# New step orders for the engines in seven kinds of stages of a sixteen-stage transformer kernel on one core

## The chip, the cores and the metric

The kernel runs on one core of a Trainium2 chip. The metric is the device time of one execution in microseconds (us). Executions of this kernel agree closely, so two versions can be told apart from about 0.2% on.

## The reference

Two blocks of a language model in fp32 over 256 tokens of width 1024. The first block is four layers, each a SwiGLU feed-forward part, a mixer and a second SwiGLU part; the mixers are a gated delta rule (layers 1 and 4), stick-breaking attention and a sparse attention. The second block is twice a three-branch mixer and a squared-ReLU feed-forward part.

```
def rmsnorm(x, g): ...
def swiglu(h, w_gu, w_down):
    gate, up = jnp.split(h @ w_gu, 2, axis=-1)
    return (jax.nn.silu(gate) * up) @ w_down
...
def gated_deltanet(h, w_in, conv_w, a_log, dt_bias, norm_g, w_out):
    # causal depthwise conv and silu on q, k, v; q and k to unit length
    # chunk_gated_delta_rule: per chunk the inverse of a unit lower
    # triangular matrix, then products with q, k, v and the state
    ...
    return o.reshape(bsz, seq, GDN_DIM).astype(h.dtype) @ w_out
...
def mixer_sublayer(x, positions, w_in, ...):
    a, b, c = gla_branch(...), gmlp_branch(...), moba_branch(...)
    return (ga * a + gb * b + gc * c) @ w_out
```

Every stage is x + part(norm(x)). The output is x after the second block.

## The kernel before

The work is cut into sixteen stages: ffn1, gdn, ffn2, ffn1, sb, ffn2, ffn1, dsa, ffn2, ffn1, gdn, ffn2, mixer2, ff2, mixer2, ff2. Activations stay in SBUF all the time; the weights come from HBM piece by piece, up to 1 MB each, through the SP queue into a ring of five buffers (`RING`). Each fp32 weight piece is split in two: ScalarE writes its rounded high part `hi` (L638), VectorE writes the rest, `lo = raw - hi` (L656); for five pieces of each gdn stage and four of the dsa stage GpSimd does that subtraction (L676, `pool_split`). The activations are split likewise (`xh`, `xl`; L720 and L812). TensorE then makes three products for each block, hi by xh, lo by xh, hi by xl (L430, L431, L432 and, for column pieces, L503 to L505). The split of piece p + 3 stands at the first step of piece p. A split has to wait until its piece has landed, and hi(q) until TensorE has used piece q - 5.

The order on every engine is written out by hand in a script for each kind of stage: a string of names such as `W x1 W gate flip turn out norm next`. `run(script, lanes)` walks it and takes the next part of the generator with that name. On all engines `W` advances the weight pieces by one step; a split is issued at the `W` at which its piece is due:

```
def run(script, lanes):
    for step in script:
        if step in lanes:
            next(lanes[step])
```

No compiler reorders anything: the instructions of an engine execute in the order of its script, and each waits for semaphores of the data that it reads and of the buffer that it overwrites. A `W` that carries no split issues nothing on ScalarE, VectorE or GpSimd.

The steps that are spoken of below:

- ffn and ff2: `x1` and `next` transpose the activation (L541, L587) and split it; `gate` is silu on ScalarE (L1113) and a product on VectorE; `flip` (L993) and `turn` (L1017, L1028) take the hidden activation through DMAs issued by GpSimd (L1005, L1009); `out` adds the residual (L836), `norm` is L867 to L882.
- gdn: `E` is one step of the convolution, one VectorE product (L1604) and six taps (L1610), with two taps on ScalarE between (L1401). `inv` on GpSimd is the inversion by 31 pairs of row operations (L1797, L1800) between a VectorE transpose (L1719) and the VectorE steps L1724, L1726, L1728 (`inv` in `vector_gdn`). ScalarE copies that inverse into block form in sixteen operations (`MT`, L1401), and from there a chain of small products (L616) and VectorE steps (L1661) leads to the stage's output. `c0` to `c3` on GpSimd (L1782, L1784) clear and mask the four blocks of the chain. The first split on GpSimd waits for the last step of the convolution, `("conv", g, 22)`.

Of the kernel before, what the change touches and what calls it, by code (L numbers as in the profile page):

```python
# [1053 lines left out]
W W W W W W W next W W  # L1054
"""
FFN_ACT = """
x1 W W W W W W W gate W W W gate W W gate W turn turn W W gate W W W W turn W gate W W turn W W W gate W W W W gate
turn W W turn gate W W W W turn W gate W W W turn W gate W W W W turn gate W W W turn W W W W turn W W W W W W W W W W
W W W W next W W
"""  # L1060
FFN_DVE = """
x1 W W W W W gate W W flip W gate W W flip W W turn gate flip W W turn W gate W flip W W W turn W W gate flip W W W
turn W gate W flip W W W turn gate W flip W W turn W gate W flip turn W gate W W flip W W turn W gate W flip W W turn
gate W flip W W turn W W W W turn W W W out W W W W W W W W W W next out out W W W W
# [98 lines left out]


# [67 lines left out]


GDN_PE = """
x1 W W rbc rbc W W W W W gates W W W gates gates gates gates W W c0 W c2 nk nk nk c3 W nk c0 nk W W c1 c2 kT c1 c3 W W
W W W W W kT W W nq nq nq W nq W W nq W W qk qk rows W W rows rows rows qk W W c2 c0 c1 c0 c2 c0 c1 c0 c2 c1 a0 c3 c2
a0 c3 a0 c3 c1 a0 a1 a0 c3 a1 a1 qk a0 a0 a1 W a1 W W a1 a1 W W W W next W gates gates nk nq
"""
GDN_ACT = """
x1 W W W rbc rbc E E ba W W gates W W E gates W W gates W W E nk E W W nk W W nk gates gates gates E nk c0 c2 nk W  # L1240
W c0 c3 c2 c1 c3 c1 W W E kT E nq E W W nq E nq nq E W W W W nq W W E kT sv W W Z rows rows c2 c0 c3 c1 Z c2 c0
rows c1 rows gate W W c3 a0 a0 a0 W W a0 a0 a1 a1 a1 a0 a0 a1 a1 a1 a1 W W W W W W next W W W gates nk nq
"""
GDN_DVE = """
x1 clear rbc W W W E E gates W W gates E gates W W gates E W W gates gates W W E c2 c0 nk nk nk nk E c0 nk c3 W W
nk c2 c1 c3 c1 W W W W inv E E gates W W E W W nq nq nq E E W W nq E W W nq nq qk qk inv c1 c2 c0 qk c3 c0 c0 c2 c1
c0 c2 c1 a0 a0 c2 c3 a0 c3 c1 a0 a1 a0 a1 c3 a0 qk a1 a0 a1 a1 a1 a1 out W W W W W W W W W W W W out next W W out W
W W rbc
# [899 lines left out]
DSA_ACT = """
W W W x1 W p0 W normq W W W turn_q W normq normq p1 W normk turn_q W normk qi turn_q W normk normk W uq index_q
index_q index index index index index W index W index uv W turn_q uk normk turn_k W attention attention attention  # L2150
attention attention attention index W attention attention attention attention attention W W W attention index W W W
next W W W
"""
# [323 lines left out]


MIXER2_PE = """
W W x1 W x1 W W gla W W W W W W decays W W W W W W W decays decays W W W W W gla W decays decays W gla gmlp W gla gmlp  # L2480
gla W gmlp gla decays gla gla W gla decays W decays gla gla decays gla gla gmlp gla W gmlp gmlp gla W W gla W gmlp W W
W gmlp gmlp moba gla W moba W moba W gmlp W W moba W W W attention attention W W W attention attention W W W W W W W
attention W W attention W W W attention W W W W W W attention W W W W yT W W W W W W yT W W W W W W next next W
"""
MIXER2_ACT = """
W W decays x1 x1 W mu W W W W W W W mz W W W W gq W W W decays decays gk W decays decays W decays decays decays W W W
gla decays W gla gg gla W gla W gelu gla gla W gmlp W gla gla gmlp W W gla gla W oq gmlp W gla gmlp moba gla W gla W
gmlp gla gmlp W ok gmlp W gla W gla ov gmlp gla moba moba W W gmlp W W W moba gmlp W W sg attention W W W attention
attention W W W W attention sg W W W sg W attention W W W W W attention W W attention W W sg attention W W W norm sg W
W W W W yT W sg W W W yT W W W W norm next next W W W norm  # L2490
"""
MIXER2_DVE = """
clear x1 x1 W W W W W W W W lr angles W W decays W W angles W decays W W decays decays W decays W W gla W decays gla
gla decays W gv W gla W gla W gla gla decays decays gla W W W gla W gla W gla gmlp gla gla W gmlp gla gmlp gmlp W gmlp
gla gla W W gmlp W W gmlp gmlp gmlp moba W moba moba gla W W W W W W moba W gmlp attention W W y W W attention
attention W W attention W y attention W W W W y W W W W W attention W y W W W W attention W attention W W y W W W yT W
W y W yT W W W W W W norm out norm W next next out W W W norm
"""


# [683 lines left out]
```

## Time and profile before

| | us |
|---|---|
| median of three runs | 2890.73 (2890.49 to 2891.34) |
| span of the profiled execution | 2888.2 |
| PE busy | 2850.4 (99%) |
| DVE busy | 1794.7 (62%) |
| ACT busy | 1577.3 (55%) |
| POOL busy | 451.5 (16%) |

The profiled execution carries no time of its own but its span, which begins with the first recorded instruction and ends with the last; the three runs stand 2.5 us above it. Start times in the views count from the start of the span. PE is TensorE, DVE VectorE, ACT ScalarE, POOL GpSimd.

### The profile page before, as it was taken

The page shows a single profiled execution, that of the slowest core. Times are in us where ns is not written, and L with a number is a line of the kernel's source. Part 1 is how long each engine was busy: PE and PEld are TensorE (multiplying, and loading weights), DVE is VectorE, ACT ScalarE, POOL GpSimd, SP SyncE. Part 2 cuts the span into 40 slices and gives each one's busy share as a digit, 9 for nine tenths or more (in the row PEclk, how much of TensorE's full clock was granted, in tenths as well). Part 3 has the DMA queues.
Part 4 walks back from the last instruction along what each step waited for, and adds up shares of the span by engine and source line. Part 5 has one row for each costly group of instructions (what it writes and reads, how often), then busy time and mean ns, then how long its engine had stood idle before and what let it go on. Part 6 is the DMA issues. An engine that isn't in the chain of part 4 may idle for free. (4 is left out here: it accounts for less than half of the span.)

```text
span 2888.2 us, 35966 instructions
## 1 busy us (share of the span) xinstructions
PE 2850.4 (99%) x14255; PEld 2416.6 (84%) x14255; DVE 1794.7 (62%) x2190; ACT 1577.3 (55%) x1982; POOL 451.5 (16%) x700
## 2 busy tenths in 40 slices
PE   9999999999999999999999999999999999999998
PEld 7889888888988888878888898888888888888887
DVE  5558666565666556466556487566675665775664
ACT  5458754544554454565444387644566463566462
POOL 1203512021002112041202107121000020000020
PEclk9999999999999999999999999999999999999999
DMA  8764277686548677537767653486645686645694
GB/s 277 233 192 144 78 217 241 194 247 214 173 153 245 214 229 237 181 117 226 227 207 242 200 160 117 136 248 211 196 147 175 209 284 220 194 146 176 217 280 158
DMA packets 397047, 574.90 MB, mean 199 GB/s; under 512 B 20016, under 2 KB 248624, under 8 KB 396880
## 3 DMA queue, kind: packets, MB, share of 16 engines
q1 hardware_dynamic: 372624, 508.62, 55.9%
q0 software_dynamic: 23680, 62.95, 7.1%
q8 instruction: 112, 1.84, 0.3%
q10 hardware_dynamic: 576, 1.05, 0.1%
q14 instruction: 55, 0.45, 0.1%
HBM read 540.03 MB, written 32.51 MB: 198 GB/s over the span
## 5 line engine op out<-in xcount | busy, mean ns | idle before, releaser
L656 DVE TENSOR_TENSOR lo<-raw,hi 128x2048 fp32r<-128x2048 f32 (+3 forms) x473 | 1050.5, 2234 | 453.7 <-ACT hi L638 453.5
L638 ACT ACTIVATE hi<-raw 128x2048 fp32r<-128x2048 f32 (+2 forms) x487 | 907.2, 1871 | 753.8 <-DMA raw<-in_ffn_w_gu 261.8
L430 PE MATMUL ps<-hi,xh 128*128 128x512 f32 (+1 forms) x2208 | 866.5, 392 | 9.5 <-DVE lo L656 7.0
L432 PE MATMUL ps<-hi,xl 128*128 128x512 f32 (+1 forms) x2208 | 859.6, 389 | 0.0
L431 PE MATMUL ps<-lo,xh 128*128 128x512 f32 (+1 forms) x2208 | 858.9, 389 | 0.0
L430 PEld LDWEIGHTS ps<-hi,xh 128*128 128x128 f32 x2208 | 415.7, 188 | 96.3 <-DVE lo L656 11.9
L432 PEld LDWEIGHTS ps<-hi,xl 128*128 128x128 f32 x2208 | 415.4, 188 | 86.0
L431 PEld LDWEIGHTS ps<-lo,xh 128*128 128x128 f32 x2208 | 415.9, 188 | 83.9 <-issue 0.5
L430 PE MATMUL ps<-hi,hhh 128*128 128x512 f32 x704 | 274.6, 390 | 0.0
L432 PE MATMUL ps<-hi,hhl 128*128 128x512 f32 x704 | 273.9, 389 | 0.0
L431 PE MATMUL ps<-lo,hhh 128*128 128x512 f32 x704 | 273.9, 389 | 0.0
L1009 POOL DMA_DIRECT2D hhr<-turned x352 | 192.1, 552 | 388.7 <-DMA turned<-hhf 379.8
L503 PE MATMUL ps<-xh,hi 128*128 128x256 f32 x672 | 193.9, 289 | 0.0
L505 PE MATMUL ps<-xh,lo 128*128 128x256 f32 x672 | 190.1, 283 | 0.0
L504 PE MATMUL ps<-xl,hi 128*128 128x256 f32 x672 | 190.1, 283 | 0.0
L1005 POOL DMA_DIRECT2D turned<-hhf x88 | 49.8, 566 | 772.1 <-DVE hhf L993 771.8
L432 PEld LDWEIGHTS ps<-hi,hhl 128*128 128x128 f32 x704 | 132.1, 188 | 27.4
L431 PEld LDWEIGHTS ps<-lo,hhh 128*128 128x128 f32 x704 | 132.2, 188 | 27.2
L430 PEld LDWEIGHTS ps<-hi,hhh 128*128 128x128 f32 x704 | 132.1, 188 | 27.2
L1113 ACT ACTIVATE sg<-ps,st 128x256 f32<-128x256 f32 x176 | 78.6, 470 | 119.9 <-PE ps L432 119.7
L1028 DVE TENSOR_TENSOR hhl<-hhr,hhh 128x512 fp32r<-128x512 f32 x88 | 60.4, 686 | 128.0 <-ACT hhh L1017 84.8
L503 PEld LDWEIGHTS ps<-xh,hi 128*128 128x128 f32 x672 | 128.8, 192 | 1.8 <-issue 1.6
(440 smaller groups left out, 3397.3 us busy)
## 6 DMA issues: line engine op xcount, KB each, us to landing
raw<-in_ffn_w_gu SPq DMA_DIRECT2D x348, 512.0 KB, 4.9
raw<-in_ffn_w_down SPq DMA_DIRECT2D x80, 1024.0 KB, 5.1
raw<-in_w_ff SPq DMA_DIRECT2D x64, 1024.0 KB, 5.6
raw<-in_w_in SPq DMA_DIRECT2D x60, 1024.0 KB, 5.3
raw<-in_gdn_w_in SPq DMA_DIRECT2D x32, 1024.0 KB, 5.6
turned<-hhf POOLq DMA_DIRECT2D x88, 256.0 KB, 4.7
hhr<-turned POOLq DMA_DIRECT2D x352, 64.0 KB, 4.0
raw<-in_sb_w_in SPq DMA_DIRECT2D x12, 1024.0 KB, 5.1
```

The costliest lines, as they stand in the source:

```text
L430: e.matmul(o, a1, r1, start=kk == 0, stop=False)
L431: e.matmul(o, a1, r2, start=False, stop=False)
L432: i = e.matmul(o, a2, r1, start=False, stop=kk == kts - 1)
L503: e.matmul(o, a1, x1, start=kk == 0 and q == 0, stop=False, skip_group_check=True)
L504: e.matmul(o, a1, x2, start=False, stop=False, skip_group_check=True)
L505: i3 = e.matmul(o, a2, x1, start=False, stop=kk == 7, skip_group_check=True)
L638: k.e.activation(k.m.hi[q % RING][:, 0:n], k.m.raw[q % RING][:, 0:n], ACT.Copy).then_inc(*k.up("act_piece_hi", ("hi", q)))
L656: k.e.tensor_tensor(m.lo[i][:, 0:n], m.raw[i][:, 0:n], m.hi[i][:, 0:n].bitcast(F32), ALU.subtract).then_inc(*k.up("dve_piece_lo", ("split" ...
L1005: k.e.dma_start(k.t["turned"][c % 4, :, 0:f.n], f.flipped[c % f.turns][:, :]).then_inc(*k.up(f"dma_send{c % 3}", ("sent", g, c), by=16))
L1009: k.e.dma_start(f.raw[32 * b:32 * b + 32, c + 1, :].rearrange("i (a r) -> i a r", a=4), rows).then_inc(*k.up(f"dma_fetch{c % 3}", *([("fet ...
L1028: k.e.tensor_tensor(f.turned(f.low, c), f.back(c), f.turned(f.high, c).bitcast(F32), ALU.subtract).then_inc(*k.up("dve_turned_lo", ("hT", ...
L1113: k.e.activation(r["sg"][i][:, :], b.ps[:, 0:256], ACT.Silu, scale=m.st[:, 16 + t:17 + t]).then_inc(*k.up("act_ffn_silu", ("silu", g, c, t)))
```

## The change

The scripts of ffn, the last ffn, ff2, gdn, dsa and mixer2 are replaced on PE, ACT and DVE, and those of gdn and dsa also on POOL. The scripts of the first stage (ffn1) and of sb are as before. No instruction is added or removed; only the order within each engine differs (the PSUM banks go with that order). One source line fewer is left after the gdn tables, so lines behind them count one less in the changed kernel. Two tables of the diff:

```diff
 FFN_LAST_PE = """
 W x1 W W W W W W W W W W W W W W W W W W W W W W W W W W W W W W W W W W W W W W W W W W W W W W W W W W W W W W W W W W
-W W W W W W W W W next next W
+W W W W W W W next W next
 """
...
 GDN_POOL = """
-clear c2 inv W W W W W W W W W W W W W W W W W W W W W W W W W W W c0 c3 c1 W W W W W W W W W W W W W W W
+clear c2 W W W W W W W W W W W W W W W W W W c0 W W W W W W W inv W W W c1 c3 W W W W W W W W W W W W W W W
```

**First place: VectorE in a gdn stage, around the transpose that feeds GpSimd's inversion.** L656 is the split of a weight piece, and its buffers turn in the ring: `lo_20`, `lo_23`, `lo_11`, `lo_14` are pieces 9, 10, 11, 12 of the stage here. L1719 (L1718 in the changed kernel) is the transpose, L1604 and L1610 (L1603, L1609) a step of the convolution. Before:

```order
L656 TENSOR_TENSOR lo_23_72<-raw_22_71,hi_24_73 128x2048
L656 TENSOR_TENSOR lo_11_60<-raw_10_59,hi_12_61 128x2048
L1719 STREAM_TRANSPOSE gow_156<-goz_155 128x1024
L1604 TENSOR_TENSOR cin_86_135<-ps,rbc_55 128x2x256
L1610 SCALAR_TENSOR_TENSOR qkv_127<-cin_86_135,vec_50,qkv_127 128x256 x6
L1604 TENSOR_TENSOR cin_84_133<-ps,rbc_55 128x2x256
L1610 SCALAR_TENSOR_TENSOR qkv_127<-cin_84_133,vec_50,qkv_127 128x256 x6
L1642 TENSOR_TENSOR ga_132<-ga_132 128x16
L656 TENSOR_TENSOR lo_14_63<-raw_13_62,hi_15_64 128x2048
```

Changed:

```order
L656 TENSOR_TENSOR lo_20_69<-raw_19_68,hi_21_70 128x2048
L656 TENSOR_TENSOR lo_23_72<-raw_22_71,hi_24_73 128x2048
L1718 STREAM_TRANSPOSE gow_156<-goz_155 128x1024
L1603 TENSOR_TENSOR cin_86_135<-ps,rbc_55 128x2x256
L1609 SCALAR_TENSOR_TENSOR qkv_127<-cin_86_135,vec_50,qkv_127 128x256 x6
L1603 TENSOR_TENSOR cin_84_133<-ps,rbc_55 128x2x256
L1609 SCALAR_TENSOR_TENSOR qkv_127<-cin_84_133,vec_50,qkv_127 128x256 x6
L656 TENSOR_TENSOR lo_11_60<-raw_10_59,hi_12_61 128x2048
```

Piece 11 has moved behind the transpose and two steps of the convolution; pieces 9 and 10 stand ahead of the transpose.

**Second place: VectorE in the same stage, from the split of piece 14 to the end of the inversion.** `lo_20` is piece 14 and `lo_23` piece 15; L1724 (L1723) is the first VectorE step behind GpSimd's inversion. Before:

```order
L1604 TENSOR_TENSOR cin_85_134<-ps,rbc_55 128x2x256
L1610 SCALAR_TENSOR_TENSOR qkv_127<-cin_85_134,vec_50,qkv_127 128x256 x6
L656 TENSOR_TENSOR lo_20_69<-raw_19_68,hi_21_70 128x2048
L1648 TENSOR_TENSOR qkv_127<-qkv_127,sy_103_152 128x512
L1604 TENSOR_TENSOR cin_86_135<-ps,rbc_55 128x2x256
L1610 SCALAR_TENSOR_TENSOR qkv_127<-cin_86_135,vec_50,qkv_127 128x256 x6
L656 TENSOR_TENSOR lo_23_72<-raw_22_71,hi_24_73 128x2048
L1648 TENSOR_TENSOR qkv_127<-qkv_127,sy_105_154 128x512
L1648 TENSOR_TENSOR qkv_127<-qkv_127,sy_102_151 128x512
L1711 TENSOR_TENSOR qkD_131<-ps,qkD_131 128x512 x2
L1724 TENSOR_SCALAR goz_155<-gov_157,const_49 128x512 x2
```

Changed:

```order
L656 TENSOR_TENSOR lo_20_69<-raw_19_68,hi_21_70 128x2048
L1647 TENSOR_TENSOR qkv_127<-qkv_127,sy_103_152 128x512
L1603 TENSOR_TENSOR cin_85_134<-ps,rbc_55 128x2x256
L1609 SCALAR_TENSOR_TENSOR qkv_127<-cin_85_134,vec_50,qkv_127 128x256 x6
L656 TENSOR_TENSOR lo_23_72<-raw_22_71,hi_24_73 128x2048
L1603 TENSOR_TENSOR cin_86_135<-ps,rbc_55 128x2x256
L1609 SCALAR_TENSOR_TENSOR qkv_127<-cin_86_135,vec_50,qkv_127 128x256 x6
L1647 TENSOR_TENSOR qkv_127<-qkv_127,sy_105_154 128x512
L1723 TENSOR_SCALAR goz_155<-gov_157,const_49 128x512 x2
```

Piece 14 now stands ahead of the last step but one of the convolution, and piece 15 ahead of the last step.

**Third place: VectorE at the end of the last ffn stage, where the first mixer2 stage takes over.** L812 writes `xl` of one token half of the next stage's input; `lo_11` is the third weight piece of mixer2. Before:

```order
L812 TENSOR_TENSOR xl_58<-ps,xh_57 128x4x128
L836 SCALAR_TENSOR_TENSOR x_56<-ps,x_56 128x512
L841 BN_STATS st_52<-x_56 128x6
L656 TENSOR_TENSOR lo_11_60<-raw_10_59,hi_12_61 128x2048
L812 TENSOR_TENSOR xl_58<-ps,xh_57 128x4x128
L867 BN_AGGR st_52<-st_52 128x2
```

Changed:

```order
L812 TENSOR_TENSOR xl_58<-ps,xh_57 128x4x128
L836 SCALAR_TENSOR_TENSOR x_56<-ps,x_56 128x512
L841 BN_STATS st_52<-x_56 128x6
L812 TENSOR_TENSOR xl_58<-ps,xh_57 128x4x128
L867 BN_AGGR st_52<-st_52 128x2
L879 SCALAR_TENSOR_TENSOR st_52<-st_52 128x1
L882 SCALAR_TENSOR_TENSOR x_56<-x_56,st_52,lrow_54 128x512 x2
L656 TENSOR_TENSOR lo_11_60<-raw_10_59,hi_12_61 128x2048
```

The second `xl` now stands ahead of the split. ScalarE's `xh` for it has moved ahead of its high part of the same piece in the same way.

## Rows read from the trace of the kernel before

**Rows 1.** The page's first part: busy us, share of the span, instructions

```profile
span 2888.2 us, 35966 instructions
PE 2850.4 (99%) x14255; PEld 2416.6 (84%) x14255; DVE 1794.7 (62%) x2190; ACT 1577.3 (55%) x1982; POOL 451.5 (16%) x700
```

**Rows 2.** Waits of PE: released by, total us, times, longest

```profile
PE ps L430 <- DVE lo L656: 7.0, 3, 3.1
PE ps L2991 <- DMA const<-in_consts: 4.3, 1, 4.3
PE ps L430 <- DVE xl L812: 2.5, 1, 2.5
PE ps L616 <- ACT zs L1401: 1.8, 2, 0.9
PE ps L616 <- ACT sl L1401: 0.9, 2, 0.4
```

**Rows 3.** Windows: us, busy of PE, PEld, DVE, ACT, POOL, clock, DMA

```profile
193.00:366.00 173.00, 166.71 (x1183) 152.99 (x1182) 130.72 (x239) 135.32 (x235) 65.48 (x77) 0.99 0.40 125
1662.00:1836.00 174.00, 166.84 (x1183) 152.85 (x1182) 133.52 (x243) 136.94 (x238) 68.61 (x78) 0.99 0.41 126
292.00:300.00 8.00, 7.99 (x33) 6.66 (x34) 7.32 (x11) 7.94 (x11) 7.06 (x14) 0.81 0.06 24
2026.00:2034.00 8.00, 6.07 (x22) 4.87 (x23) 4.14 (x9) 2.90 (x4) 0.00 (x0) 0.79 0.53 137
```

**Rows 4.** Timeline of DVE, first gdn stage: start us, us, instruction, [idle before]

```profile
254.57 4.48 DVE L656 TENSOR_TENSOR lo<-raw,hi 128x2048 fp32r<-128x2048 f32 x2
259.62 1.25 DVE L1719 STREAM_TRANSPOSE gow<-goz 128x1024 f32<-128x1024 f32 x1 [0.56 <-ACT goz L1401]
...
269.32 2.28 DVE L656 TENSOR_TENSOR lo<-raw,hi 128x2048 fp32r<-128x2048 f32 x1
...
273.98 3.56 DVE L1610 SCALAR_TENSOR_TENSOR qkv<-cin,vec,qkv 128x256 f32<-128x256 f32 x6 [1.78 <-ACT qkv L1401]
...
286.47 3.12 DVE L1610 SCALAR_TENSOR_TENSOR qkv<-cin,vec,qkv 128x256 f32<-128x256 f32 x6 [0.58 <-ACT qkv L1401]
289.52 2.43 DVE L656 TENSOR_TENSOR lo<-raw,hi 128x2048 fp32r<-128x2048 f32 x1
...
294.00 2.55 DVE L1610 SCALAR_TENSOR_TENSOR qkv<-cin,vec,qkv 128x256 f32<-128x256 f32 x6 [0.68 <-ACT qkv L1401]
...
301.60 5.59 DVE L1724 TENSOR_SCALAR goz<-gov,const 128x512 f32<-128x512 f32 x2
307.22 1.25 DVE L1726 STREAM_TRANSPOSE gow<-goz 128x1024 f32<-128x1024 f32 x1
308.50 0.69 DVE L1728 TENSOR_TENSOR gow<-gow 128x512 f32<-128x512 f32 x1
```

**Rows 5.** Timeline of POOL, same stage

```profile
288.87 0.45 POOL L1800 TENSOR_TENSOR gov<-gov,junkp 128x96 f32<-128x96 f32 x1
...
289.88 2.29 POOL L1800 TENSOR_TENSOR gov<-gov,junkp 128x91 f32<-128x91 f32 x1
...
299.48 5.07 POOL L676 TENSOR_TENSOR lo<-raw,hi 128x2048 fp32r<-128x2048 f32 x1
```

**Rows 6.** Timelines of PE and of ACT, same stage

```profile
270.79 0.60 PE L616 MATMUL ps<-const,qkv 128*128 128x128 f32 x4
...
292.01 0.79 PE L430 MATMUL ps<-hi,xh 128*128 128x512 f32 x1 [3.08 <-DVE lo L656]
...
318.85 2.43 PE L616 MATMUL ps<-sl,sl 128*128 128x128 f32 x17 [0.44 <-ACT sl L1401]
...
309.23 7.25 ACT L1401 ACTIVATE sl<-gow 32x128 f32<-32x128 f32 x16 [0.72 <-DVE gow L1728]
```

**Rows 7.** Timelines of DVE and of ACT, last ffn stage into mixer2

```profile
2024.89 2.29 DVE L656 TENSOR_TENSOR lo<-raw,hi 128x2048 fp32r<-128x2048 f32 x1 [0.69 <-ACT hi L638]
2027.10 0.68 DVE L812 TENSOR_TENSOR xl<-ps,xh 128x512 fp32r<-128x512 f32 x1
...
2022.87 1.92 ACT L638 ACTIVATE hi<-raw 128x2048 fp32r<-128x2048 f32 x1 [1.31 <-DMA raw<-in_w_in]
2024.69 0.58 ACT L720 ACTIVATE xh<-ps 128x512 fp32r<-128x512 f32 x1
```

**Rows 8.** The page's costliest groups: count, then busy us, mean ns

```profile
L656 DVE TENSOR_TENSOR lo<-raw,hi 128x2048 fp32r<-128x2048 f32 (+3 forms) x473 | 1050.5, 2234 | 453.7 <-ACT hi L638 453.5
L638 ACT ACTIVATE hi<-raw 128x2048 fp32r<-128x2048 f32 (+2 forms) x487 | 907.2, 1871 | 753.8 <-DMA raw<-in_ffn_w_gu 261.8
```

**Rows 9.** Windows of PE alone: an ffn stage, the stretch of mixer2 and ff2

```profile
366.00:560.00 194.00, 194.00 (x874) 1.00 0.72 220
2450.00:2700.00 250.00, 249.89 (x1304) 1.00 0.56 178
```

More of the change, by code:

```diff
@@ L1053 @@
 W x1 W W W W W W W W W W W W W W W W W W W W W W W W W W W W W W W W W W W W W W W W W W W W W W W W W W W W W W W W W
-W W W W W W W next W W
+W W W W W next W W W W
 """
 FFN_ACT = """
-x1 W W W W W W W gate W W W gate W W gate W turn turn W W gate W W W W turn W gate W W turn W W W gate W W W W gate
-turn W W turn gate W W W W turn W gate W W W turn W gate W W W W turn gate W W W turn W W W W turn W W W W W W W W W W
-W W W W next W W
+x1 W W W W W W gate W W gate W W W W W turn W gate W W W turn gate W W turn W gate W W W turn W W W W W gate W gate W
+turn W turn gate W W turn W W W gate W gate W turn W W W W W gate W turn W turn W W W W W W W turn W W W W W W W W W W
+W W W next W W
 """
 FFN_DVE = """
-x1 W W W W W gate W W flip W gate W W flip W W turn gate flip W W turn W gate W flip W W W turn W W gate flip W W W
-turn W gate W flip W W W turn gate W flip W W turn W gate W flip turn W gate W W flip W W turn W gate W flip W W turn
-gate W flip W W turn W W W W turn W W W out W W W W W W W W W W next out out W W W W
+x1 W W W gate W W W W gate W W W flip W flip W gate flip W turn W turn gate W W W W W W flip gate W flip W W turn gate
+W W flip W turn W gate turn W W flip W turn gate W W W flip turn W W W gate W W flip gate W W turn W flip W turn W W
+gate flip W W turn W W W W W turn W W W W out W W W W W W W W W next out out W W W
 """
@@ L1234 @@
 GDN_PE = """
-x1 W W rbc rbc W W W W W gates W W W gates gates gates gates W W c0 W c2 nk nk nk c3 W nk c0 nk W W c1 c2 kT c1 c3 W W
-W W W W W kT W W nq nq nq W nq W W nq W W qk qk rows W W rows rows rows qk W W c2 c0 c1 c0 c2 c0 c1 c0 c2 c1 a0 c3 c2
-a0 c3 a0 c3 c1 a0 a1 a0 c3 a1 a1 qk a0 a0 a1 W a1 W W a1 a1 W W W W next W gates gates nk nq
+rbc W nk x1 W W rbc W W W gates gates W W W gates W W gates W W gates nk c0 c2 nk c3 nk nk W nk c2 nq c1 W c0 W c3 kT
+c1 kT W W W W W W W W nq W nq nq W W W W qk W nq qk gates W rows W rows W W c1 qk c0 c2 c3 c0 c2 rows c0 rows c1 c0 c2
+c1 a0 c3 a0 c2 a0 c1 c3 a0 a1 a0 a1 c3 a0 a1 qk a0 a1 a1 a1 W W W a1 W W W W nq next gates W
 """
 GDN_ACT = """
-x1 W W W rbc rbc E E ba W W gates W W E gates W W gates W W E nk E W W nk W W nk gates gates gates E nk c0 c2 nk W
-W c0 c3 c2 c1 c3 c1 W W E kT E nq E W W nq E nq nq E W W W W nq W W E kT sv W W Z rows rows c2 c0 c3 c1 Z c2 c0
-rows c1 rows gate W W c3 a0 a0 a0 W W a0 a0 a1 a1 a1 a0 a0 a1 a1 a1 a1 W W W W W W next W W W gates nk nq
+a1 rbc W x1 W W rbc E ba W E W W gates W W W gates E gates E a0 W gates W gates nk E nk nk nk nk c2 c0 E W W W W c2 c3
+c0 c1 c3 c1 W E gates W W kT E W W W kT W E nq nk E nq W W nq W W nq E W W W E sv Z nq rows gates rows c1 c2 c0 c3 Z
+c0 c2 c1 c3 nq W rows rows W gate W a0 a0 a0 W a0 W a1 a0 a1 a0 W a1 W a1 W a1 W a1 W next W W W
 """
 GDN_DVE = """
[L1245 to L1248, printed above, removed]
+nk nk x1 W clear nq W rbc W E E W gates W W gates W E gates E gates W W W gates W E gates nk c2 nk c0 nk E W c2 c3 nk
+c0 c1 c3 c1 W W W inv W E E nq W E W W W E W nq W W nq E W W E W W nq inv nq gates qk qk W c0 c1 c2 W W W qk c0 W c2
+c0 c1 W c0 rbc c3 a0 c2 a0 c1 c3 c2 a0 c1 c3 a0 a1 a0 a1 c3 a0 a1 qk a1 W W W a0 a1 a1 a1 W W out W next out W out W W
 """
 GDN_POOL = """
-clear c2 inv W W W W W W W W W W W W W W W W W W W W W W W W W W W c0 c3 c1 W W W W W W W W W W W W W W W
+clear c2 W W W W W W W W W W W W W W W W W W c0 W W W W W W W inv W W W c1 c3 W W W W W W W W W W W W W W
 """
@@ L2147 @@
+W attention attention index W attention attention attention W attention W W W next index index W W
 """
 DSA_ACT = """
[L2149 to L2152, printed above, removed]
+W W W x1 W p0 normq W normq W normq W W W p1 index_q W turn_q normk qi normk W W normk W turn_q uq W W index_q W
@@ L2153 @@
+turn_q index index normk index index uv index index W W W turn_q uk turn_k attention attention attention attention
+attention attention W attention attention index attention attention attention W W attention W W W normk next W index W
+index
 """
 DSA_DVE = """
-normk x1 W normq W W normq W W W W W normq W normk W W normk normk index_q normk W turn_q W W index turn_q index index
-index index index W index W index index attention attention attention W attention attention W attention W turn_q
-attention attention attention attention index_q attention attention W out W W W W next out turn_q out W W W
+normq normk x1 W W W W normq W W W normq W W W normk index_q W normk W normk turn_q normk W turn_q index W index index
@@ L2158 @@
+W turn_q index index index index index W index W attention attention attention attention attention attention W
+attention attention W W attention attention index_q attention W attention out W W W next turn_q W out W W out
 """
 DSA_POOL = """
-W W W W W W W W W W W W W attention W W W attention attention attention attention attention attention W attention
-attention W attention W attention W W W attention W W W W W
+W W W W attention W W W W W W W W W W W W W attention attention attention attention attention attention attention
@@ L2162 @@
+attention W W W W W W attention W attention W W W attention
 """
@@ L2479 @@
 MIXER2_PE = """
[L2480 to L2483, printed above, removed]
+W W gla gmlp x1 W x1 W W W W gmlp gmlp W W W W W decays W W W W W W W W gla W decays decays W W W gla decays W gmlp W
@@ L2484 @@
+gla moba gla gla gla gla W W W W gmlp gla W gmlp decays gla W gla W moba gla decays W W moba gmlp W gla W moba gla W W
+gla gmlp W gla decays gla attention W decays gmlp W attention W W gmlp W W attention W W W W W W W W W W attention W W
+W attention attention W W decays W W W attention W attention W W W W W W yT W W W W yT W W W W W W next next W
 """
 MIXER2_ACT = """
-W W decays x1 x1 W mu W W W W W W W mz W W W W gq W W W decays decays gk W decays decays W decays decays decays W W W
-gla decays W gla gg gla W gla W gelu gla gla W gmlp W gla gla gmlp W W gla gla W oq gmlp W gla gmlp moba gla W gla W
@@ L2491 @@
+W W W ok W gla moba gmlp W gla moba gla ov gla W gla moba gmlp gla W W W sg W W gmlp attention W W W gmlp W W W
+attention W sg W sg W W W W attention W attention attention norm sg W W W attention W W W W attention W W W W
+attention sg W W W yT sg W W W yT W W W norm W W next next W W norm W
 """
 MIXER2_DVE = """
-clear x1 x1 W W W W W W W W lr angles W W decays W W angles W decays W W decays decays W decays W W gla W decays gla
-gla decays W gv W gla W gla W gla gla decays decays gla W W W gla W gla W gla gmlp gla gla W gmlp gla gmlp gmlp W gmlp
@@ L2495 @@
-gla gla W W gmlp W W gmlp gmlp gmlp moba W moba moba gla W W W W W W moba W gmlp attention W W y W W attention
-attention W W attention W y attention W W W W y W W W W W attention W y W W W W attention W attention W W y W W W yT W
-W y W yT W W W W W W norm out norm W next next out W W W norm
+x1 W W clear x1 W W W W W W lr W decays W decays decays W decays W decays decays W W W angles gla W W W gla W decays W
+decays gv gla W angles gla gla gla W W gla gmlp gla W gmlp W gmlp W W W gla gla W W W gla gmlp W gmlp moba W gla moba
@@ L2498 @@
+gmlp gla W gmlp W moba W gla gla W gla W gmlp moba gla attention W W decays W W W attention W W gmlp W W W y W gmlp
+attention W W y W y W W W attention W W attention W y attention W W W attention W W W W W attention W y W yT W W y W
+yT W W W norm W W W out W norm W next W next out W W norm
 """
```

38 lines of the change are left out of this document (18 added, 20 removed).

## The prediction

> **What bounds the kernel.** I read the page first: PE is busy for 2850.4 of 2888.2 us, DVE for 62%, ACT for 55% [rows 1]. The span can only shrink where PE is idle or slowed, or grow where a new order makes PE idle. So the question is where those 37.8 idle us lie. The windows by stage answer it: an ffn stage (366 to 560) and the stretch of the later mixer2 and ff2 stages (2450 to 2700) have PE busy from end to end [rows 9]; the two gdn stages lack 6.3 and 7.2 us each [rows 3]. The list of PE's waits names the causes: three waits for the low part of a weight piece, 7.0 us with a longest of 3.1, one wait of 2.5 us for `xl`, 4.3 us for the first constants (not touched), and pieces of under 1 us for the gdn chain, such as `zs` and `sl` [rows 2]. The reader should see that about 12 us lie in three places that the change moves: piece 14 in each gdn stage, and the entry into mixer2. The tail behind the last matmul, some 8 us, keeps its order.
>
> A wait also costs clock. After the 3.08 us of idle time at 292.01 [rows 6], the window 292 to 300 shows a granted clock of 0.81; after the wait for `xl` the window 2026 to 2034 shows 0.79 [rows 3], that is a part of each at the lower level of 1.2 GHz and the rest at 2.4. 0.19 and 0.21 of 8 us mean that 1.5 and 1.7 us' worth of full-speed clocks were lost in each.
>
> **Entry into mixer2 (once).** Before, DVE does the split of the third mixer2 piece (2024.89 to 2027.18) ahead of the second `xl`, and that split had to wait for the high part, which began at 2022.87, when its DMA had landed; `xh` came only behind it, at 2024.69 [rows 7]. PE sat idle for 2.5 us [rows 2]. Now `xh` and `xl` go first: `xl` needs 0.58 + 0.68 us after its transpose and no piece. PE's next wait can only be the split itself. It now stands behind the statistics and two L882 operations, so it ends some 2 us later than 2027.2; I allow 0.9 us for that, between 0 (PE has two steps of other work first) and 2. Gain: 2.5 + 1.7 - 0.9 = 3.3 us, bounds 2 and 4.2.
>
> **Each gdn stage (twice).** There are three edits that count.
>
> (a) *Piece 14 goes ahead of a convolution step.* In the trace its split runs from 289.52, and PE waits 3.08 us for it [rows 4, 6]. Moved ahead of one step (the taps alone were 3.12 us just before it [rows 4]) it is done in time: 3.1 us of idle time and 1.5 us of clock go away at that place.
>
> (b) *Piece 11 goes behind the transpose and two steps.* Before, pieces 10 and 11 are split from 254.57, 4.48 us for both [rows 4]. Now 9 and 10 are there, and 11 begins only where piece 12 did, at about 269.3, and ends at 271.7. PE had its `kT` product at 270.79, between the two steps (24 matmuls, 2.9 us each) of that piece [rows 6]; that product and other small ones now stand ahead of it, so PE asks for piece 11 between 268 and 270. I take 270, since more work stands ahead of it: a new wait of 1.7 us, bounds 0 and 3.5, with or without a clock loss of up to 1.5.
>
> (c) *The inversion and what follows.* DVE's transpose still waits for ACT's `goz` at 259.62 [rows 4], so GpSimd's 62 operations start as before, at 261. Each of them that meets a split is long: 0.45 us became 2.29 beside the split at 289.52 [rows 5]. Four splits fell into the inversion before (pieces 12 to 15), now five do: + 1.9 us, end at 301.4 instead of 299.5. The convolution ends later too: before, its last six taps start at 294.00 and end at 296.5, with piece 15 behind them [rows 4]; now pieces 11, 14 and 15 all stand ahead of that end, so it comes by (at most) 3 x 2.3 us later, less the 1 us of a product that moved behind: about 302.3. The GpSimd split of piece 16 waits for that last step, so it starts at 302.3 and not at 299.48 [rows 5]. DVE's L1724 is held by it: two 512-wide operations took 5.59 us, the first up to the end of the split at 304.55, where other operations of that size take 0.69 [rows 4]. DVE reaches L1723 now at about 303.3, again inside the split. So the inverse is ready 9.7 us after the split's start, as before (309.2 - 299.5): at 312.0, + 2.8 us. MT follows (7.25 us for sixteen operations), and then the first product of the chain on PE, which was at 318.85 [rows 6]: now at 321.7.
>
> The Trainium skill, "SBUF — State Buffer", its part on the engine ports, says that VectorE and GpSimd share one port pair as an exclusive lock, held for a whole instruction, and that the loser blocks. The trace agrees on both sides: 2.29 us against 0.45, and 3.7 us for the first L1724. The case in which this rule decides is (c) and the second rival.
>
> PE was dense up to 317 before, with 0.9 us for `zs` and 0.4 for `sl` in each stage [rows 2]: its own work and the chain met. Now PE's work is done earlier (a) and the chain comes later (c), so the chain sets the end: **+ 2.8 us** for the stage, whatever (a) gave. The wait that was at 292 reappears ahead of the chain, in pieces of 2 to 5 us between the transposes of the blocks, and with it a slow clock of 0 to 2 us; I take 1. Two groups of transposes (`rows`) moved from ahead of the chain into it, and one product from behind a weight step to ahead of it: 0 to 2 us, I take 0.3 since the chain is full of DVE gaps. Sum for a gdn stage: 2.8 + 1.0 + 0.3 = 4.1, bounds - 2 (c is covered by the time from a) and + 7. Two stages: **+ 8.2**.
>
> **The rest.** Ten of the other stages are taken together. In the six ffn stages a split stands at least 1.7 steps of 2.7 us ahead of its use, and a split costs 1.87 us on ACT and 2.23 on DVE [rows 8], so I find no new wait: 0, bounds 0 and 1 each. In the last ffn stage two `gate` steps stand together on ACT ahead of a high part: ACT is held until PE has finished the second one's product, then 0.9 us of silu, 1.87 and 2.23 make 5.0 us against the 5.4 that PE needs for two steps: covered, by 0.4 us only; 0 to 1. The dsa stage keeps its top-k chain; a low part less early, - 1 to + 1. In mixer2 and ff2, which had PE busy for 249.89 of 250 us [rows 9], nothing is left to gain and a wait here and there can arise: 0 to 2 for all four, I take 0.5.
>
> **Sum**: - 3.3 + 8.2 + 0.5 = + 5.4 on the profiled span of 2888.2, so 2893.6; the median of the runs stands 2.5 us above that span, which gives **2896.1**. That is + 0.19%, just inside the 0.2% (5.8 us) that a measurement of this kernel can tell from no change.
>
> **Rivals.**
> 1. *The order of the gdn stage wins.* If conv's end and the inversion are not later (the splits fill gaps in which DVE waited for ACT: 0.58 us ahead of most groups of taps, and 1.78 once [rows 4]), (a) is a real gain: 3.1 + 1.5 per stage less 1.7 for (b), twice 2.9, and 3.3 at mixer2: - 9 us, 2881.6. For it: PE's longest waits go. Against it: one more split inside the inversion. Chance 0.17, all of it faster.
> 2. *GpSimd's split and the later steps hit harder (the slower side).* The place is the wait of GpSimd for the last convolution step and DVE's L1723 behind it. If PE's idle time ahead of the chain reaches 3 us at once, it costs clock as at 292 (1.5 us), and if (b) does so too, another 1.5; with the chain at + 4 that is 7 us a stage: + 14 - 3.3 + 0.5 = + 11, 2902. It decides from an inverse ready later than about 313. For it: the two waits of 3.1 and 2.5 us both lost clock. Chance 0.26, all of it slower.
> 3. *The change hides itself*: each new wait is as long as the one it replaces, in the gdn stages and at mixer2. 2890.7, chance 0.15, all of it within 0.2%.
>
> **How the numbers follow.** The forecast case (a sum between - 2 and + 9) has 0.42; its middle lies just inside the bound of 5.8 us, and two thirds of it, 0.28, below that bound. Faster by over 0.2%: 0.17 (rival 1). Within 0.2%: 0.28 + 0.15 = 0.43. Slower: the other 0.14 and rival 2, 0.40. The range runs from 2882 (rival 1) to 2908 (rival 2 with its bound of 7 us a stage and 3 of the rest).
>
> **What would show it.** In the changed profile: no wait for `xl` at the mixer2 entry and a clock above 0.95 there; no 3 us wait for the low part of piece 14, but one of 1 to 2 us for piece 11 near 270; the inversion of 261 ending at 301, the GpSimd split of piece 16 starting at 302 and not 299.5; the sixteen MT operations starting at 312; waits of PE on ACT's MT or `sl` of 2 to 5 us. I am wrong if MT starts before 310 (rival 1), if the entry keeps its wait, or if an ffn or mixer2 stage shows PE waits of over 3 us.

## The result

The changed kernel takes 2909.88 us (2905.88 to 2915.58, four runs) against 2891.03 us (2890.49 to 2891.99) of the kernel before: ratio 1.0065, interval 1.0054 to 1.0077, so it is slower by 18.9 us. The forecast was 2896.1 us with a range to 2908: the side was the one that its sum pointed to, the size is over three times as large, and the time lies above the range. Five of the later executions, which took 3964 to 12405 us, are left out of all medians below.

The page of the changed kernel:

```profile
span 2908.9 us, 35971 instructions
PE 2855.8 (98%) x14255; PEld 2423.4 (83%) x14255; DVE 1813.3 (62%) x2190; ACT 1574.5 (54%) x1982; POOL 451.8 (16%) x700
```

Against [rows 1] the span has grown by 20.7 us and PE's busy time by 5.4 us with the same 14255 matmuls; the rest is idle time of PE. DVE is busy for 18.6 us more with the same number of instructions: single operations have become long, not more.

Where it was lost is read from one group of rows that stands at the head of each stage, the transposes of its input on PE (`next` and `x1`; start us, us). In the kernel before:

```profile
372.90 1.04 PE L587 MATMUL ps<-const,x 128*128 128x128 f32 x8
...
1207.12 1.04 PE L587 MATMUL ps<-const,x 128*128 128x128 f32 x8
...
1302.68 1.04 PE L587 MATMUL ps<-const,x 128*128 128x128 f32 x8
...
1843.96 1.04 PE L587 MATMUL ps<-const,x 128*128 128x128 f32 x8
...
2273.41 1.03 PE L541 MATMUL ps<-const,x 128*128 128x128 f32 x8
...
2700.65 1.03 PE L541 MATMUL ps<-const,x 128*128 128x128 f32 x8
```

and in the changed one:

```profile
378.97 1.04 PE L587 MATMUL ps<-const,x 128*128 128x128 f32 x8
...
1213.19 1.04 PE L587 MATMUL ps<-const,x 128*128 128x128 f32 x8
...
1318.46 1.04 PE L587 MATMUL ps<-const,x 128*128 128x128 f32 x8
...
1865.24 1.04 PE L587 MATMUL ps<-const,x 128*128 128x128 f32 x8
...
2291.30 1.03 PE L541 MATMUL ps<-const,x 128*128 128x128 f32 x8
...
2718.83 1.03 PE L541 MATMUL ps<-const,x 128*128 128x128 f32 x8
```

The lag between them is a ledger of the stages:

| stretch | lag at its end, us | its own share | forecast |
|---|---|---|---|
| up to the end of the first gdn stage | 6.1 | + 6.1 | + 4.1 |
| ffn2, ffn1, sb, ffn2, ffn1 | 6.1 | 0.0 | 0 |
| dsa | 15.8 | + 9.7 | 0, between - 1 and + 1 |
| ffn2, ffn1, second gdn | 21.3 | + 5.5 | + 4.1 |
| last ffn, first mixer2 | 17.9 | - 3.4 | - 3.3 |
| ff2, second mixer2 | 18.2 | + 0.3 | } + 0.5 |
| last ff2 | 20.7 | + 2.5 | } |

So half of the loss is in a stage of 96 us for which the forecast had nothing. PE's waits in the changed kernel:

```profile
PE ps L616 <- issue: 8.1, 2, 4.3
PE ps L2214 <- ACT drl L2245: 7.2, 1, 7.2
PE ps L503 <- DVE lo L656: 4.2, 2, 2.1
...
PE ps L430 <- DVE xl L812: 2.0, 2, 1.0
PE ps L430 <- DVE lo L656: 1.8, 3, 0.9
...
PE ps L430 <- DVE fhl L1028: 1.4, 1, 1.4
```

The three waits of [rows 2] that the change aimed at have gone (7.0 us for L656 is 1.8, and the 2.5 us for `xl` at mixer2 is now two of 1.0 elsewhere). In their place stand one of 7.2 us in dsa, two of up to 4.3 us ahead of the gdn chain, and two of 2.1 us for piece 11 in gdn.

**The dsa stage.** GpSimd's and DVE's timelines of the changed kernel:

```profile
1244.67 10.53 POOL L676 TENSOR_TENSOR lo<-raw,hi 128x2048 fp32r<-128x2048 f32 x2 [81.67 <-ACT hi L638]
```

```profile
1244.24 0.69 DVE L2382 COPY dkT<-ps 128x512 f32<-128x512 f32 x1
1244.84 6.00 DVE L656 TENSOR_TENSOR lo<-raw,hi 128x1536 fp32r<-128x1536 f32 x1
1250.77 4.58 DVE L2101 TENSOR_TENSOR drt<-dq,const 128x128 f32<-128x128 f32 x1
1255.27 0.28 DVE L2102 TENSOR_TENSOR drt<-dq,const 128x128 f32<-128x128 f32 x1
```

GpSimd does two splits back to back, 1244.67 to 1255.20. DVE's split of 1536 elements begins behind the first and takes 6.00 us, and the next product of 128 elements takes 4.58 us. The pair on GpSimd is longer too, 10.53 us. It begins when ACT has written the high part of its first piece (the releaser in the row), 31 us into the stage instead of 42. In the kernel before the same two DVE operations and the same pair on GpSimd read:

```profile
1239.16 1.75 DVE L656 TENSOR_TENSOR lo<-raw,hi 128x1536 fp32r<-128x1536 f32 x1
...
1241.95 0.28 DVE L2102 TENSOR_TENSOR drt<-dq,const 128x128 f32<-128x128 f32 x1
```

```profile
1248.87 9.16 POOL L676 TENSOR_TENSOR lo<-raw,hi 128x2048 fp32r<-128x2048 f32 x2 [95.10 <-ACT hi L638]
```

There the pair stood beside the top-k, whose MAX8 kept their length:

```profile
1249.32 0.61 DVE L2425 MAX8 st<-dwk 128x8 f32<-128x128 f32 x2
```

Now DVE is held for (6.00 - 1.75) + (4.58 - 0.28) = 8.6 us ahead of the scoring of the heads, ACT waits 8.80 us for it, and PE 7.25 us for ACT, with the granted clock at its lower level behind that (0.50 in the window below):

```profile
1257.58 0.80 PE L2214 MATMUL ps<-dkT,dqiT 128*128 128x128 f32 x2 [7.25 <-ACT drl L2245]
```

The window behind it (columns as in [rows 3]):

```profile
1254.00:1262.00 8.00, 4.42 (x12) 3.69 (x13) 7.74 (x22) 3.05 (x7) 1.20 (x1) 0.50 0.00 1
```

**The gdn stage** of the changed kernel, DVE, GpSimd and ACT, against [rows 4 to 6]:

```profile
268.87 2.46 DVE L656 TENSOR_TENSOR lo<-raw,hi 128x2048 fp32r<-128x2048 f32 x1
...
301.28 7.10 DVE L1723 TENSOR_SCALAR goz<-gov,const 128x512 f32<-128x512 f32 x2 [0.81 <-POOL gov L1799]
...
309.69 4.89 DVE L1727 TENSOR_TENSOR gow<-gow 128x512 f32<-128x512 f32 x1
```

```profile
301.13 4.61 POOL L676 TENSOR_TENSOR lo<-raw,hi 128x2048 fp32r<-128x2048 f32 x1
...
309.49 4.55 POOL L676 TENSOR_TENSOR lo<-raw,hi 128x2048 fp32r<-128x2048 f32 x1
```

```profile
314.62 7.09 ACT L1400 ACTIVATE sl<-gow 32x128 f32<-32x128 f32 x16 [6.72 <-DVE gow L1727]
```

The reader should see two holds on the way from the inversion to MT, not one: the first split on GpSimd holds L1723, as before, and the second, which starts 0.2 us ahead of L1727, holds that one for 4.2 us. The second split starts early because `c0`, which stood between the two splits, has moved ahead of the inversion.

### The profile page after: what moved, and what is told of

Same layout as the page of the kernel before. It is cut to its first block, busy times and chain, and to the rows that moved or that the text cites. A ratio compares the mean times of both kernels' runs of the same rounds, so it can differ in the third digit from the quotient of the medians.

```text
span 2908.9 us, 35971 instructions
## 1 busy us (share of the span) xinstructions
PE 2855.8 (98%) x14255; PEld 2423.4 (83%) x14255; DVE 1813.3 (62%) x2190; ACT 1574.5 (54%) x1982; POOL 451.8 (16%) x700
## 4 chain that ended last, share of the span: by engine, by line
PE 88%; DVE 4%; ACT 4%; DMA 2%; POOL 1%; issue 1%; SPq 0%; DVEq 0%; ACTq 0%; POOLq 0%
PE ps L430 26%; PE ps L432 26%; PE ps L431 26%; PE ps L616 3%; PE ps L503 1%; PE ps L505 1%; PE ps L504 1%; DVE lo L656 1%; ACT hi L638 1%; POOL gov L1799 1%; ACT goz L1400 1%; DVE qkv L1609 1%; PE ps L587 1%; PE ps L603 1%; DMA raw<-in_w_ff 1%
## 5 line engine op out<-in xcount | busy, mean ns | idle before, releaser
L656 DVE TENSOR_TENSOR lo<-raw,hi 128x2048 fp32r<-128x2048 f32 (+3 forms) x473 | 1055.4, 2245 | 441.9 <-ACT hi L638 441.1
L1132 DVE SCALAR_TENSOR_TENSOR hhb<-ps,st,sg 128x256 f32<-128x256 f32 x176 | 78.0, 477 | 184.2 <-ACT sg L1113 184.2
```

The lines of the kernel that those rows point to most:

```text
L656: k.e.tensor_tensor(m.lo[i][:, 0:n], m.raw[i][:, 0:n], m.hi[i][:, 0:n].bitcast(F32), ALU.subtract).then_inc(*k.up("dve_piece_lo", ("split" ...
L1132: k.e.scalar_tensor_tensor(r["f"].put(c, t), b.ps[:, 256:512], m.st[:, 16 + t:17 + t], r["sg"][i][:, :], ALU.mult, ALU.mult).then_inc(*k.u ...
```

## The experiments

Each run is given as its difference to the runs of the kernel before on the same chip (2890.94, 2891.19, 2891.38 and 2891.10 us in the four groups: e1 to e4, e5 to e7, e8 to e10, e12). What is said to come back is the 18.9 us less that difference.

**e1: dsa scripts back.** `DSA_PE`, `DSA_ACT`, `DSA_DVE` and `DSA_POOL` of the changed kernel are those of before.

> The changed kernel with the four dsa scripts of the kernel before; all else as changed. In the two traces the dsa stage grew by 9.7 us (start of the ffn2 part behind it: 1302.68 against 1318.46, where the start of dsa had 1207.12 against 1213.19). Theory: those 9.7 us are the dsa scripts' own, so the run comes out 9.7 us below the changed kernel (about 2900), with DVE's 1536-wide split back at 1.75 us. Rival: the dsa stage is slow because it starts at another moment (weights landing at other times); then less than 3 us come back.

Measured: 2900.5 us, + 9.6; ratio 1.0032 (1.0019 to 1.0045). That is 9.3 us less than the changed kernel: the theory holds, the loss goes with the scripts.

**e2: GpSimd's dsa splits later, nothing else.**

```diff
-    run(script, {"W": pool_pieces(k, plan, si.g), "attention": pool_attention(...)})
+    run(script, {"W": pool_pieces(k, plan, si.g, ("scored", si.g, 7)), "attention": pool_attention(...)})
```

> The changed kernel with one edit: GpSimd's four splits of the dsa stage wait for DVE's scoring of the eighth head. Nothing else moves on any engine. Theory: DVE's split of 6.00 us and its rotary product of 4.58 us (1.75 and 0.28 before) were held by the two GpSimd splits; with them later both are back below 2 and 0.3 us, PE's wait of 7.2 us for the relu goes, and 7 to 9.7 us come back (2900 to 2903). Rival: the new order on PE, ACT and DVE is itself late (the rotary steps stand behind the split and the heads are taken apart); then the wait stays above 4 us and 0 to 2 us come back, or the run is slower since the low parts come later.

Measured: 2902.74 us, + 11.8 (ratio 1.0041, 1.0027 to 1.0056): 7.1 us came back with the order on PE, ACT and DVE as changed. DVE's rows:

```profile
1245.25 1.75 DVE L656 TENSOR_TENSOR lo<-raw,hi 128x1536 fp32r<-128x1536 f32 x1
...
1254.08 4.69 DVE L2419 TENSOR_TENSOR dsc<-dsc,const 128x128 f32<-128x128 f32 x1
```

```profile
1253.92 9.30 POOL L676 TENSOR_TENSOR lo<-raw,hi 128x2048 fp32r<-128x2048 f32 x2 [90.82 <-DVE dsc L2414]
```

The split is back at 1.75 us and PE's 7.2 us wait is gone. One hold is left: the pair starts at 1253.92, and the next product of two SBUF tiles that DVE comes to takes 4.69 us instead of 0.28 or so. It delays the top-k, and PE waits 6.2 us in one piece where 2.3 stood. So the dsa loss is the place of the GpSimd pair relative to DVE's two-input operations; what is left against e1 is 2.2 us (11.8 against 9.6), that hold included, and the two intervals overlap.

**e3: gdn scripts back.**

> The changed kernel with the four gdn scripts of the kernel before. The two gdn stages grew by 6.1 and 5.5 us in the traces. Theory: 11.6 us come back, about 2898. Rival: part of it is owed to the ffn stages that stand around them, then 6 us or less.

Measured: 2897.31 us, + 6.4 (1.0022, 1.0013 to 1.0031): 12.5 us back. No part of the ffn stages around gdn can be seen in it.

**e4: the kernel before with the last ffn's scripts.**

> The kernel before with only the three scripts of the last ffn stage as changed. Theory: PE's 2.5 us wait for xl and the slow clock behind it go, nothing replaces them: 3.4 us faster than before, about 2887.5. Rival: the gain in the trace of the changed kernel came from the new mixer2 scripts; then 0 to 1 us.

Measured: 2888.06 us, - 2.9 (0.9990, 0.9980 to 0.9999). The wait for `xl` is gone; the only one left there is the 0.6 us that PE waits for the split behind it:

```profile
2025.24 0.67 DVE L812 TENSOR_TENSOR xl<-ps,xh 128x512 fp32r<-128x512 f32 x1
...
2028.52 2.28 DVE L656 TENSOR_TENSOR lo<-raw,hi 128x2048 fp32r<-128x2048 f32 x1
```

**e5: the second hold in gdn.** In the changed kernel, `c0` behind `c3`, so that the second split comes later.

```diff
-clear c2 W W W W W W W W W W W W W W W W W W c0 W W W W W W W inv W W W c1 c3 W ...
+clear c2 W W W W W W W W W W W W W W W W W W W W W W W W W inv W W W c1 c3 c0 W ...
```

> The changed kernel with one step of GpSimd's gdn script moved: c0 stands behind c3, ahead of the second split (piece 17), where the changed script has it ahead of the inversion. Theory: in the changed trace the second split began at 309.49, 0.2 us ahead of DVE's L1727, which then took 4.89 us instead of 0.69; with c0 in between the split begins 2 us later, L1727 takes 0.7 us, the inverse is ready 4.2 us earlier and the two stages give back 3 us each or a little more: 6 to 8 us, about 2903. Rival: L1727 is long for another reason, or MT then waits for c0 on GpSimd: 0 to 2 us.

Measured: 2907.64 us, + 16.5 (1.0055, 1.0040 to 1.0070): 2.4 us back, not 6 to 8, and its interval overlaps that of the changed kernel. In the two traces the gdn stages give 0.3 and 0.0 us of it; the dsa stage, which the edit does not touch, is 1.3 us shorter, with a granted clock of 0.81 instead of 0.72 from 1246 to 1264. The profile says why gdn gives so little:

```profile
309.00 0.96 DVE L1727 TENSOR_TENSOR gow<-gow 128x512 f32<-128x512 f32 x1
309.88 1.79 DVE L1647 TENSOR_TENSOR qkv<-qkv,sy 128x512 f32<-128x512 f32 x1
311.60 4.49 DVE L1641 TENSOR_TENSOR ga<-ga 128x16 f32<-128x16 f32 x1
316.01 1.27 DVE L1710 TENSOR_TENSOR qkD<-ps,qkD 128x512 f32<-128x512 f32 x2
```

```profile
311.09 4.96 POOL L676 TENSOR_TENSOR lo<-raw,hi 128x2048 fp32r<-128x2048 f32 x1
```

L1727 is short again and MT begins at 309.99, 4.6 us earlier, as expected. But the split now holds the next two-input operation, a sum of 16 elements that took 0.16 us and takes 4.49; behind it stands L1710, for which PE waits 3.4 us:

```profile
316.74 2.08 PE L616 MATMUL ps<-qkv 128*128 128x128 f32 x8 [3.42 <-DVE qkD L1710]
```

The first gdn stage wins 0.3 us of the 4.6. The hold was moved, not removed.

**e6: piece 14 earlier, in the kernel before** (edit a of the prediction alone).

```diff
 GDN_ACT
-... nq E nq nq E W W W W nq ...
+... nq E nq nq W W E W W nq ...
 GDN_DVE
-... nq nq nq E E W W nq E ...
+... nq nq nq E W W E nq E ...
```

> The kernel before with one thing moved in gdn: the high and low part of piece 14 stand ahead of E's last step but one on ACT and DVE (the changed kernel's edit a, alone). PE's wait of 3.1 us at 292 should go. Theory of the prediction (the chain from the inversion sets the stage's end, whatever PE gained ahead of it): 0 to 2 us faster for both stages together, and the idle time reappears ahead of the chain near 317. Rival (the wait at 292 is a real loss): 3.1 + 1.5 us a stage, 9 us faster in all.

Measured: 2896.73 us, + 5.5 (1.0017, 1.0008 to 1.0026): slower, which neither expectation had. PE's 3.1 us wait for the piece went, but DVE came to the split before ACT's high part was there, and the convolution ended at 299.2 instead of 296.5:

```profile
287.50 2.29 DVE L656 TENSOR_TENSOR lo<-raw,hi 128x2048 fp32r<-128x2048 f32 x1 [2.16 <-ACT hi L638]
...
309.72 1.25 DVE L1726 STREAM_TRANSPOSE gow<-goz 128x1024 f32<-128x1024 f32 x1
```

L1726 was at 307.22 in [rows 4], and the stage grew by 3.3 us. GpSimd is done with the inversion at 297.3 and waits 1.98 us for the convolution. Then its split begins 0.2 us behind DVE's split of piece 15:

```profile
299.09 2.28 DVE L656 TENSOR_TENSOR lo<-raw,hi 128x2048 fp32r<-128x2048 f32 x1
...
299.25 7.81 POOL L676 TENSOR_TENSOR lo<-raw,hi 128x2048 fp32r<-128x2048 f32 x1 [1.98 <-DVE qkv L1610]
```

It ends at 307.06 where it ended at 304.55, the same 2.5 us by which L1726 is later. So the edit makes the inverse later, by way of a hold in the other direction, and that is what the theory had missed. Since both moved at once, the run does not show what the wait at 292 is worth alone.

**e7: ff2 scripts, in the kernel before.**

> The kernel before with only the three ff2 scripts as changed. In the trace of the changed kernel the last stage grew by 2.5 us and the ff2 before it by 0.4, with PE waits for xl (1.0 each) and for the low part of the hidden activation (1.4). Theory: these scripts cost 2 to 3 us by themselves, about 2893.5. Rival: the last stage was late because of the mixer2 scripts ahead of it; then within 1 us of before.

Measured: 2893.28 us, + 2.1; ratio 1.0004 (0.9994 to 1.0014). The middle is as the theory had it, the interval takes in no change, so this part is likely and not shown by the times.

**e8: no GpSimd split between the inversion and MT.** In the changed kernel piece 16 goes to DVE, and GpSimd's other four splits wait for the inverse.

```diff
-                self.pool |= {q for p in own for q in self.due(p) if 13 <= p - own[0] <= 17}
+                self.pool |= {q for p in own for q in self.due(p) if 14 <= p - own[0] <= 17}
...
-    run(script, {"W": pool_pieces(k, plan, g, ("conv", g, 22)), "clear": ...})
+    run(script, {"W": pool_pieces(k, plan, g, ("U", g)), "clear": ...})
```

> The changed kernel with two edits in gdn: piece 16 is split by DVE (right behind the last convolution step) and no more by GpSimd, and GpSimd's other splits (17 to 20) wait until DVE has finished the inverse. Theory: then no DVE step between the inversion and MT is held: L1723 takes 1.4 us for both instead of 7.10, L1727 0.7 instead of 4.89, MT starts near 306 instead of 314.6, and each gdn stage gets 6 to 8 us shorter: 2894 to 2898. Rival: the new order itself is late and the holds cost little; then MT starts a few us earlier but the stages win under 2 us each.

Measured: 2897.68 us, + 6.3 (1.0023, 1.0013 to 1.0032): 12.6 us back, all that the gdn scripts had cost.

```profile
303.27 2.06 DVE L1723 TENSOR_SCALAR goz<-gov,const 128x512 f32<-128x512 f32 x2 [0.48 <-POOL gov L1799]
305.37 1.25 DVE L1725 STREAM_TRANSPOSE gow<-goz 128x1024 f32<-128x1024 f32 x1
306.65 0.96 DVE L1727 TENSOR_TENSOR gow<-gow 128x512 f32<-128x512 f32 x1
```

```profile
308.29 7.24 ACT L1400 ACTIVATE sl<-gow 32x128 f32<-32x128 f32 x16
```

MT starts 6.3 us earlier than in the changed kernel, with that kernel's scripts on all engines, and the first gdn stage is 6.2 us shorter. The two L1723 still take 2.06 us for the 1.4 of the expectation; GpSimd's mask product L1783 runs beside the second (303.59, 1.46 us). L1641 is still held (4.58 us), but PE waits for its follower only 1.2 us in one of the two stages.

**e9: only ffn, last ffn and mixer2 stay changed.**

> The changed kernel with the scripts of gdn, dsa and ff2 from the kernel before; what is left of the change are ffn, the last ffn and mixer2. Theory: parts add up, ffn and mixer2 are worth nothing, the last ffn 3.4 us: about 2887.5, like the run with the last ffn's scripts alone. Rival: ffn or mixer2 are worth something: outside 2885 to 2890.

Measured: 2887.89 us, - 3.5 (0.9988, 0.9979 to 0.9998), the same as e4 within the intervals: the new ffn and mixer2 scripts are worth nothing that can be measured.

**e10: the parts that pay, put together.** The last ffn's, ffn's and mixer2's new scripts, dsa and ff2 as before, gdn new with the two edits of e8.

> The changed kernel with dsa and ff2 from the kernel before and both edits of the run without holds in gdn. Theory: PE's 3.1 us wait at 292 is gone, the chain starts earlier than before, the entry to mixer2 is 3.4 us shorter: 2881 to 2886, faster than both kernels. Rival: PE's new waits in gdn (piece 11, 2.1 us, and the small ones behind the chain, 2.3 us) eat the gain: 2887 to 2890.

Measured: 2887.44 us, - 3.9 (0.9985, 0.9975 to 0.9994). It is faster than both kernels, but not than e9, and lies where the rival had it. PE waits in each gdn stage for piece 11 (2.1 us) and behind the chain (1.4 + 0.9 us), and at piece 11 it loses clock as well (columns as in [rows 3]; the changed kernel ahead, e10 behind):

```profile
270.00:278.00 8.00, 6.01 (x48) 5.81 (x48) 7.42 (x9) 6.70 (x10) 7.29 (x10) 1.00 0.42 131
...
270.00:278.00 8.00, 6.85 (x44) 6.85 (x45) 7.42 (x10) 6.70 (x9) 7.30 (x10) 0.79 0.42 131
```

The second stage shows 0.79 at that place too (1742 to 1750). That these waits use up what gdn gains is read from the list; no run tests it by itself.

**e12: piece 11 earlier, on top of e10.**

```diff
 GDN_DVE
-... W W W inv W E E nq W E W ...
+... W W W inv W E W E nq E W ...
```

> The run e10 with one more edit: on DVE the split of piece 11 stands between the two convolution steps behind the transpose, not behind both. ACT's high part of that piece was ready at 263.9. Theory: PE's wait of 2.1 us for piece 11 goes in both gdn stages, and since the chain is no longer late there the stages keep most of it: 1 to 4 us below e10 (2887.4), so 2883.5 to 2886.5. Rival: the chain takes it back as in the run with the earlier split of piece 14: within 1 us of e10.

Measured: 2891.60 us, + 0.5 (1.0001, 0.9992 to 1.0011), 4.4 us worse than e10. PE's wait for piece 11 went, and in its place:

```profile
279.13 1.19 PE L1328 MATMUL ps<-sy,const 128*128 128x512 f32 x1 [4.11 <-ACT sy L1400]
```

DVE was 2.4 us later with the next convolution step, and all behind it: ACT's `sy`, and the end of the convolution (301.0 instead of 299.6). The granted clock from 278 to 286 was 0.59. Which share of the 4.4 us belongs to PE's longer wait, to its clock and to the later convolution was not separated; in common with e6 is that DVE had no time to spare ahead of the inverse.

**e11: the kernel before with the last ffn's scripts and the two edits of e8.** It was expected at 2885 to 2887 us if the chain gives back only the waits ahead of it, and below 2883 if the chain alone had set the end of the stage. It has no time: in the old order DVE's `W` for piece 16 stands behind the inverse, and the engines wait for each other for ever. So what the old gdn order would gain without the holds stays open.

## Why the prediction was wrong

The clause that failed is in "The rest": "The dsa stage keeps its top-k chain; a low part less early, - 1 to + 1." It measured + 9.7 us (e1: 9.3). The clause asks only when the low parts are ready. It does not ask what DVE does during the 9 us of GpSimd's pair, although (c) uses just this rule. What the runs showed in its place is DVE held for 8.6 us by that pair and PE idle for 7.25 us behind it, with the clock at 0.50. An estimate from the rows of before, made after the fact, would have been two GpSimd splits of about 4.6 us, each met by a two-input operation: some 8 us. With that the sum is + 13, and a range of the same width would have held the time. None of the signs of being wrong that the prediction lists came up (MT before 310, the entry's wait, a wait of over 3 us in ffn or mixer2): the list had no sign for dsa.

The second term that was too small is that of the gdn stages, 4.1 us each where 6.1 and 5.5 were measured; the causes are under (c).

The other steps, in their order:

- *Entry into mixer2*: forecast - 3.3, in the trace - 3.4, alone - 2.9 (e4). The new wait for the split was 0.6 us where I allowed 0.9.
- *(a) piece 14*: the wait at 292 went, and the stage gained nothing by it, as forecast. e6 made this edit alone, but the inverse came later with it, so what (a) is worth with the inverse in its old place is not shown.
- *(b) piece 11*: forecast a wait of 1.7 us near 270; it is 2.09 us at 271.39, with the split ending at 271.3 (forecast 271.7). No clock was lost at it in this profile (1.00 from 270 to 278). In the profiles of e1, e2, e5, e8 and e10, with the same wait at the same place, that window shows 0.79, so the clock loss of up to 1.5 us, which the prediction left open, came in those.
- *(c)*: the inversion ends at 301.1 (forecast 301.4), with five splits inside. The convolution ended at 299.8, not 302.3: piece 14 had stood ahead of that end before as well (289.52 in [rows 4]), so two splits were new there and not three, and the one idle time of 1.78 us ahead of taps shrank to 0.58; the other idle times of 0.58 stayed. GpSimd's split started at 301.13 for 302.3. The inverse was ready at 314.6 instead of 312.0, since a second hold, that of L1727 by the second split, was not in the sum: 4.2 us. GpSimd's `c0` had moved ahead of the inversion, so that split came earlier: the same omission as in dsa. The clock cost more than the 1 us I took: the window 316 to 324 shows 0.65, some 2.8 us' worth, behind a wait of 4.28 us. A stage cost 6.1 and 5.5 us, forecast 4.1, bound 7.
- *ffn, last ffn's inside, mixer2*: nothing, as forecast (0.0 us over the five stages between gdn and dsa, and e9). *ff2* (the paragraph speaks of ten stages and lists twelve): with mixer2 2.8 us where the bound was 2, most of it in the last stage, with waits of 1.0 and 1.4 us.
- *Rival 2* named the right place and the right sign; its point of decision, an inverse later than 313, was passed by 1.6 us. But it priced the clock and not the second hold, and it had no word on dsa. That the forecast had the right sign is owed to gdn alone.

## What to carry to other kernels

When an order changes, lay the long operations of GpSimd beside what DVE does in the same stretch before asking who waits for their results: a 4.6 us GpSimd subtraction held a DVE sum of 16 elements for 4.5 us. Moving the GpSimd operation a little only changes the victim (e5); what worked was to have none between two points of the critical chain (e8). And the longest wait in the list need not be worth its length: two attempts to remove one by doing a split earlier made the kernel slower (e6 against the kernel before, e12 against e10), since what stood behind that split on DVE came later.

## What the runs showed of the hardware

- DVE operations with two inputs in SBUF, and L1723 with one (TENSOR_SCALAR), are held until GpSimd's running subtraction ends: 6.00 us for 1.75, 4.58 for 0.28, 4.89 for 0.69, 4.49 for 0.16, and two L1723 7.10 for 2.06 (e8). Beside the same subtractions, MAX8 and products that read one input from PSUM (L1711 in the kernel before, 0.69 us inside the subtraction of [rows 5]) kept their length. This is what the Trainium skill states in "SBUF — State Buffer", in the part on engine ports; I had not expected that operations of 16 elements pay the same price as those of 1536.
- It goes the other way too: in e6 the first GpSimd split began 0.2 us behind a DVE split and took 7.81 us instead of 4.61. The 3.2 us more reach to about 302.5, the end not of that split (301.4) but of the two products of two SBUF tiles that DVE did right behind it (L1648, to 302.57); that GpSimd was held through all three is an estimate from these rows.
- The same wait of PE can cost clock or not: behind 2.1 us at 271.4 the window 270 to 278 shows a granted clock of 1.00 in one profile and 0.79 in five.
- The changed kernel's four runs lie 9.7 us apart, those of the kernel before 1.5; but 21 later runs of the kernel before spread over 6.7 us, so that the change scatters more is likely and not shown. What a hold costs depends on which of two operations starts first, by some 0.2 us at L1727; neither this nor the clock was shown to be the reason for the scatter.
